# Interleaving two accumulation groups, matmul by matmul, in the value projection and in the memory's key/value projection of a two-layer decoder kernel

## What is computed

```python
mk_p, mv_p = mem_kv(mem_prompt, w_mem_kv[l])    # 256 memory rows -> 512 key and 512 value columns
...
proj = x @ w_in
cb, cc, ch, rq, rk, rv, rg, mq, gl = jnp.split(proj, split_idx, axis=-1)
v = rv.reshape(b, t, RET_HEADS, RET_DV)          # 1024 value columns of the retention branch
q = rotary(rq.reshape(...), pos);  k = rotary(rk.reshape(...), pos) * (RET_DK ** -0.5)
o, new_state = retention(q, k, v, ret_state)
...
m_out = mem_attention(mq.reshape(...), mk, mv).reshape(b, t, MEM_WIDTH) @ w_mem_out
```

## Time and profile before

| | |
|---|---|
| runs of the kernel before | 2145.36, 2146.7, 2146.8 us (median 2146.7) |
| the profiled execution's own time | 2146.93 us |
| its span, from first to last instruction | 2145.1 us |
| PE busy | 2124.1 us (99%) |
| PE's weight loads busy | 2062.7 us (96%) |
| DVE, ACT, POOL busy | 1046.5 (49%), 524.5 (24%), 1310.6 us (61%) |
| mean granted clock of PE | 0.998 |

### The profile page before, as it was taken

The page is one execution under the profiler, slowest core; times in us unless marked ns, Lnnn a source line. Parts: engine busy times, 40 slices in busy tenths (PEclk is TensorE's granted clock), DMA queues, the critical chain, the costliest instruction groups (busy, mean ns, idle before and its releaser), DMA issues.

```text
span 2145.1 us, 38116 instructions
## 1 busy us (share of the span) xinstructions
PE 2124.1 (99%) x15716; PEld 2062.7 (96%) x15716; DVE 1046.5 (49%) x1669; ACT 524.5 (24%) x935; POOL 1310.6 (61%) x1549
## 2 busy tenths in 40 slices
PE   8999999999999999999999999999999999999997
PEld 8898999999999999999998989999999999999997
DVE  6156300543268873626781571006424787726257
ACT  4121021031014141414241210210410141514133
POOL 6744657645683947466757346676456748475574
PEclk9999999999999999999999999999999999999999
DMA  5415324234332323222323153332352313222331
GB/s 175 130 55 171 124 80 137 70 108 155 101 99 60 99 79 99 80 81 80 97 72 118 58 177 107 110 118 70 111 175 79 99 58 101 79 80 79 99 99 45
DMA packets 200315, 215.26 MB, mean 100 GB/s; under 512 B 5600, under 2 KB 192992, under 8 KB 200160
## 3 DMA queue, kind: packets, MB, share of 16 engines
q1 hardware_dynamic: 170688, 172.84, 25.6%
q10 hardware_dynamic: 29472, 40.20, 5.5%
HBM read 199.06 MB, written 13.97 MB: 99 GB/s over the span
## 4 chain that ended last, share of the span: by engine, by line
PE 96%; DVE 3%; ACT 0%; DMA 0%; issue 0%; POOL 0%; ACTq 0%; DVEq 0%
PE gp L578 53%; PE gp L1107 12%; PE gp L604 9%; PE gp L594 7%; PE qb L684 7%; PE gp L758 3%; PE qb L758 2%; PE gp L936 1%; PE gp L948 1%; PE qb L724 1%; DVE r L2157 1%; DVE x_lo L2063 0%; DVE r L2057 0%; DVE r L2054 0%; DVE m_lo L1665 0%; DVE m_hi L1664 0%
## 5 line engine op out<-in xcount | busy, mean ns | idle before, releaser
L466 POOL TENSOR_TENSOR w_lo<-stage,w_hi 128x256 fp32r<-128x256 f32 x1008 | 812.5, 836 | 92.0 <-ACT w_hi L1201 71.7
L463 POOL TENSOR_SCALAR w_hi<-stage 128x1024 fp32r<-128x1024 f32 x240 | 256.1, 1067 | 511.1 <-PE gp L578 257.1
L578 PE MATMUL gp<-b_hi,w_hi 128*128 128x288 f32 x1408 | 303.8, 297 | 0.0
L578 PE MATMUL gp<-x_hi,w_hi 128*128 128x288 f32 x1408 | 303.8, 298 | 0.0
L578 PE MATMUL gp<-x_lo,w_hi 128*128 128x288 f32 x1408 | 301.2, 295 | 0.0
L578 PE MATMUL gp<-x_hi,w_lo 128*128 128x288 f32 x1408 | 301.1, 295 | 0.0
L578 PE MATMUL gp<-b_lo,w_hi 128*128 128x288 f32 x1408 | 300.6, 295 | 0.0
L578 PE MATMUL gp<-b_hi,w_lo 128*128 128x288 f32 x1408 | 300.6, 295 | 0.0
L578 PEld LDWEIGHTS gp<-b_hi,w_hi 128*128 128x128 f32 x1408 | 226.6, 188 | 3.4 <-issue 3.1
L578 PEld LDWEIGHTS gp<-x_hi,w_hi 128*128 128x128 f32 x1408 | 226.8, 189 | 2.9 <-issue 2.6
L578 PEld LDWEIGHTS gp<-x_lo,w_hi 128*128 128x128 f32 x1408 | 226.7, 189 | 0.0
(11 more groups left out here) (299 smaller groups left out, 4272.9 us busy)
## 6 DMA issues: line engine op xcount, KB each, us to landing
stage<-in_w_in SPq DMA_DIRECT2D x54, 1024.0 KB, 5.9
stage<-in_w_up SPq DMA_DIRECT2D x32, 1024.0 KB, 5.4
stage<-in_w_down SPq DMA_DIRECT2D x32, 1024.0 KB, 5.2
stage<-in_w_in SPq DMA_DIRECT2D x40, 256.0 KB, 4.0
stage<-in_w_ret_out SPq DMA_DIRECT2D x8, 1024.0 KB, 5.3
stage<-in_w_mem_kv SPq DMA_DIRECT2D x8, 1024.0 KB, 5.2
stage<-in_w_out SPq DMA_DIRECT2D x8, 1024.0 KB, 5.2
s_in_c<-in_ret_state ACTq DMA_DIRECT2D x8, 512.0 KB, 5.1
```

What stands on the lines that cost most here:

```text
L463: nc.gpsimd.tensor_scalar(hi, raw, 1.0, 1.0, ALU.mult, ALU.mult).then_inc(hi_done, 1)
L466: ins = nc.gpsimd.tensor_tensor(lo[:, k:k + 2, :], raw[:, k:k + 2, :], hi[:, k:k + 2, :].bitcast(F32), ALU.subtract)
L578: last = mm(gp[:, 2 * (i % 2) + half, 0:HALF], w[:, i % 4, k * P:(k + 1) * P], x(k, half), start=(n == 0), stop=(n == 3 * nk - 1))
```

## The change

Nothing is computed that was not before, and no matmul is added or removed. The order of matmuls on PE changes in both projections, and with it the places where PE waits. In V the five token tiles become the groups (1, 2), (3, 4), (0) for `j` = 0 and (3, 1), (2, 4), (0) for `j` = 1, and within a group the two tiles, and so their banks, alternate from one matmul to the next. Among the key tiles, K0 and K1 alternate, then K2 and K3; for these pairs PE first waits for both weight tiles and for both pairs of banks. Among the value tiles the two halves of the memory rows alternate. ACT, DVE, POOL and SP keep their code.

```diff
-                    for t in (1, 2, 3, 4, 0) if j == 0 else (3, 1, 2, 4, 0):
+                    for tiles in ((1, 2), (3, 4), (0,)) if j == 0 else ((3, 1), (2, 4), (0,)):
                         if s == 0:
-                            if j == 0 and t in (1, 3):
-                                pe.wait_ge(pair_free[t // 2], l * (TILES // 2) + T_RV // 2 + 1)
-                            elif j == 0 and t == 0:
-                                take(l, 0, ("v", 0))
-                            elif j == 1 and t in (1, 2, 3):
-                                take(l, (2, 3, 1)[t - 1], ("v", 1))
-                            elif j == 1 and t == 4:
-                                pe.wait_ge(pair_free[1], l * (TILES // 2) + T_RV // 2 + 3)
+                            for t in tiles:
+                                if j == 0 and t in (1, 3):
+                                    pe.wait_ge(pair_free[t // 2], l * (TILES // 2) + T_RV // 2 + 1)
+                                elif j == 0 and t == 0:
+                                    take(l, 0, ("v", 0))
+                                elif j == 1 and t in (1, 2, 3):
+                                    take(l, (2, 3, 1)[t - 1], ("v", 1))
+                                elif j == 1 and t == 4:
+                                    pe.wait_ge(pair_free[1], l * (TILES // 2) + T_RV // 2 + 3)
...
                         for k in (2 * s, 2 * s + 1):
...
-                            for n, (x, w) in enumerate(terms):
-                                last = mm(value_bank(j, t), x, value_rows(w, s, k % 2), start=(k == n == 0),
-                                          stop=(k == KT - 1 and n == len(terms) - 1))
...
+                            for n in range(3 if tiles[0] else 2):
+                                for t in tiles:
...
+                                    end = k == KT - 1 and n == (2 if t else 1)
+                                    last = mm(value_bank(j, t), x, value_rows(w, s, k % 2), start=(k == n == 0), stop=end)
+                                    if end and j == 1 and t in (1, 2, 3):
+                                        last.then_inc(side_full[(2, 3, 1)[t - 1]], 1)
+                                    elif end and t == 4:
+                                        last.then_inc(values_done, 1)
...
             pe.wait_ge(mem_split, l + 1)
-            for i in range(4):
+            for i in (0, 2):
                 t = T_KV + i
-                pe.wait_ge(split_done, l * TILES + t + 1 + RING)
-                pe.wait_ge(pair_free[i % 2], l * (TILES // 2) + t // 2 + 1)
-                n = 0
+                pe.wait_ge(split_done, l * TILES + t + 2 + RING)
+                for bank in range(2):
+                    pe.wait_ge(pair_free[bank], l * (TILES // 2) + t // 2 + 1)
                 for k in range(KT):
-                    for w, x in ((w_hi, mt_hi), (w_hi, mt_lo), (w_lo, mt_hi)):
-                        last = mm(gp[:, 2 * (i % 2), 0:ML], w[:, i, k * P:(k + 1) * P], x[:, k, :],
-                                  start=(n == 0), stop=(n == 3 * KT - 1))
-                        n += 1
-                last.then_inc(tile_done, 1)
+                    for n, (w, x) in enumerate(((w_hi, mt_hi), (w_hi, mt_lo), (w_lo, mt_hi))):
+                        for j in range(2):
+                            last = mm(gp[:, 2 * j, 0:ML], w[:, i + j, k * P:(k + 1) * P], x[:, k, :],
+                                      start=(k == n == 0), stop=(k == KT - 1 and n == 2))
+                            if k == KT - 1 and n == 2:
+                                last.then_inc(tile_done, 1)
             for i in (0, 2):
                 t = T_KV + 4 + i
                 pe.wait_ge(split_done, l * TILES + t + 2 + RING)
                 pe.wait_ge(pair_free[i // 2], l * (TILES // 2) + (T_KV + 4) // 2 + 1)
-                for m in range(2):
-                    n = 0
-                    for k in range(KT):
-                        for x, w in ((mt_hi, w_hi), (mt_hi, w_lo), (mt_lo, w_hi)):
+                for k in range(KT):
+                    for n, (x, w) in enumerate(((mt_hi, w_hi), (mt_hi, w_lo), (mt_lo, w_hi))):
+                        for m in range(2):
```

More of the change, by code:

```diff
@@ L739, in _ @@
                     pe.wait_ge(split_done, l * TILES + T_RV + 4 * j + s + 1 + RING)
-                    for t in (1, 2, 3, 4, 0) if j == 0 else (3, 1, 2, 4, 0):
+                    for tiles in ((1, 2), (3, 4), (0,)) if j == 0 else ((3, 1), (2, 4), (0,)):
                         if s == 0:
-                            if j == 0 and t in (1, 3):
-                                pe.wait_ge(pair_free[t // 2], l * (TILES // 2) + T_RV // 2 + 1)
-                            elif j == 0 and t == 0:
-                                take(l, 0, ("v", 0))
-                            elif j == 1 and t in (1, 2, 3):
-                                take(l, (2, 3, 1)[t - 1], ("v", 1))
-                            elif j == 1 and t == 4:
-                                pe.wait_ge(pair_free[1], l * (TILES // 2) + T_RV // 2 + 3)
-                        first = NS + (t - 1) * P
-                        for k in (2 * s, 2 * s + 1):
[L752 to L756, removed]
-                            for n, (x, w) in enumerate(terms):
-                                last = mm(value_bank(j, t), x, value_rows(w, s, k % 2), start=(k == n == 0),
-                                          stop=(k == KT - 1 and n == len(terms) - 1))
[L760 to L764, removed]
@@ new lines, in _ @@
+                        for k in (2 * s, 2 * s + 1):
+                            for n in range(3 if tiles[0] else 2):
+                                for t in tiles:
+                                    cols = slice(NS + (t - 1) * P, NS + t * P)
+                                    if t == 0:
+                                        x, w = x_short[:, k, :], (w_hi, w_lo)[n]
+                                    else:
+                                        x, w = ((x_hi, x_hi, x_lo)[n][:, k, cols], (w_hi, w_lo, w_hi)[n])
+                                    end = k == KT - 1 and n == (2 if t else 1)
[4 more added lines that the diff above has]
+                                        last.then_inc(values_done, 1)
@@ L943, in _ @@
                 pe.wait_ge(pair_free[i // 2], l * (TILES // 2) + (T_KV + 4) // 2 + 1)
-                for m in range(2):
-                    n = 0
-                    for k in range(KT):
-                        for x, w in ((mt_hi, w_hi), (mt_hi, w_lo), (mt_lo, w_hi)):
+                for k in range(KT):
+                    for n, (x, w) in enumerate(((mt_hi, w_hi), (mt_hi, w_lo), (mt_lo, w_hi))):
+                        for m in range(2):
                             last = mm(gp[:, i + m, 0:2 * P], x[:, k, m * P:(m + 1) * P],
-                                      w[:, i:i + 2, k * P:(k + 1) * P], start=(n == 0), stop=(n == 3 * KT - 1))
-                            n += 1
+                                      w[:, i:i + 2, k * P:(k + 1) * P], start=(k == n == 0), stop=(k == KT - 1 and n == 2))
                 last.then_inc(tile_done, 2)
```

## The result

The changed kernel takes 2160.46 us (2158.9 to 2160.96, 4 runs) against 2146.75 us before: a ratio of 1.0063, 95% interval 1.0051 to 1.0076, 13.7 us slower. The forecast was 2157.5 with a range from 2152.5 to 2161.5. The profiled execution is the quickest of the four, 2158.9 us with a span of 2157.1 us, 12.0 us above that of before.

The account below looks back on a forecast made before the run. PE, busy 99% of the span, was taken as the bound. With 0 for distance and V, KV's 2 x 5.4 = 10.8 us on the profiled 2146.93 gave 2157.7, so 2157.5 us for the median; range 2152.5 to 2161.5.

Parts of the forecast that it names:

- The distance does not change: V and KV: matmuls stay 226.7 and 120.0 ns apart, since alternating banks buys nothing; counted as 0.
- KV: 5.4 us a layer in four gaps: KV: four new PE waits in each layer, 1.1 + 2.4 + 0.7 + 1.2 us.
- The second: Start of K2 and K3: PE waits for ACT's copy of K1, behind ACT's weight tile for M0; 2.4 us.
- The fourth: Start of M2 and M3: PE waits for POOL's low parts of both; 1.1 to 1.2 us.
- third: Start of M0 and M1: PE waits for ACT's copy of K2; 0.7 us, POOL's low part just in time.
- The first gap: Start of K0 and K1: PE waits for DVE's L1869 to leave pair 1; 1.1 us.
- V costs 0: V: the regrouped tiles add no PE wait; cost 0.
- its cover is over 2 us: End of V: outputs(0) has over 2 us to spare behind ACT's later copies; if gone, at most 1 us a layer.
- The clock: Rival: the clock falls in KV's new gaps, about 2.5 us a stretch; 2162.5 with one per layer; chance 5%.
- the worse rate in the 576 matmuls of the MLP: Shifted PE phase may switch 576 matmuls from 130.0 to 133.3 ns: 1.9 us a layer, 3.8 us in the range, unsummed.
- a wait in V that I cost at 0: Rival: only V or KV differs, by a V wait or the worse rate in the 576: 2159 to 2162; chance 7%.
- The rate of stretches: A stretch's matmul distance can differ by 3.3 ns without reason in the code; about 3 us either way, range only.

Follow-up runs that it names:

- experiment 6: Against the kernel before, only the two halves of KV's value tiles alternate; key tiles and V as before: 2146.77 us, ratio 1.000.
- experiment 4: The change's KV with the V of before, and ACT makes both key copies ahead of the two high-part weight tiles: 2155.08 us, ratio 1.0044.
- experiment 5: The change's KV with the V of before, and the four key tiles have four banks of their own: 2152.31 us, ratio 1.0028.
- KV alone: The change's KV with the V of the kernel before: 2158.7 us, ratio 1.0059.
- experiment 7: Kernel before, but in usual tiles (L578, no wait inside) all matmuls of one token half precede the other's, 24 in a row per bank: 2143.66 us.
- experiment 8: Kernel before, but the usual tile (L578) takes its two halves in the order 0, 1, 1, 0: 2157.49 us, ratio 1.0051.
- experiment 9: Kernel before, but in the usual tile (L578) the bank changes after every third matmul: 2150.36 us, ratio 1.0018.
- experiment 10: Kernel before, with 24 matmuls in a row per bank in usual tiles, except 12 first-MLP-group tiles that keep alternating: 2141.23 us, ratio 0.9974.

## Why the prediction was right, and where it was not

- *The distance does not change.* Right, and shown: 226.7 ns in V after the change, 120.0 ns in experiment 6. The 13.3 ns over the columns are there with either order. What they are is not settled.
- *KV: 5.4 us a layer in four gaps.* Right in place, releaser and order, and 5.2 us measured. The sum's terms hold the slower first distance too; with it the gaps are 1.2, 2.2, 0.7 and 1.05 for its 1.1, 2.4, 0.7 and 1.2. The second is shorter since ACT's copy of K1 starts 0.1 us before the end of its weight tile (318.61 against 318.71) and takes 0.36 us, and its release is sooner than I had allowed. The fourth is shorter since POOL's two low parts took 5.60 us (for 5.7). Experiments 4 and 5 show the second, third and fourth causes apart: ACT's written order, then the copies, then the weights of M0 to M3. The first gap, DVE's, is read from the trace and stays in every run with this KV; no experiment removed it.
- *V costs 0.* Wrong. The step that failed is "its cover is over 2 us": I followed what waits for ACT's copies down to `outputs(0)` along `v`, and did not follow DVE, which behind its own addition from `v_low` clears `S`, scales `qd` and makes `sc`, the other operand of the same matmuls. That chain's cover was under 0.1 us. The term is 1.4 us a layer in place of 0; the bound for it, "at most that 1 us", was short too, since `qd` took 1.22 us for 0.69 behind POOL.
- *The clock.* A rival at 5%, and it happens: 1.5 us a time behind the gap of 2.2 us, by the mean clocks in two of four runs of the change and in all of KV alone, but not as often in the change nor as dear as priced. I had set that gap beside an idle of 7.0 us and one of 0.4 us, and no row stood between.
- *Together.* The profiled execution is 12.0 us longer: 2 x 5.2 us in KV and 2 x 1.4 in V, less the 1.4 us won ahead of the first V, and 0.2 us spread over the rest. The median is 13.7 us longer, with a fall of the clock in half of the runs. The forecast had 10.8.
- *The range.* That 2160.46 lies inside it is in part luck. Its upper end stood for the worse rate in the 576 matmuls of the MLP, and these kept their 130.0 ns (74.88 us); what raised the time was the wait in V and the clock, and the sum had neither. The wait in V stood among the rivals, "a wait in V that I cost at 0", at 7%, and the measured median lies in that rival's 2159 to 2162.
- *The rate of stretches.* I had kept it out of the sum as chance. Experiment 5 suggests that it can differ between executions of one program (768 matmuls, 130.0 or 133.3), and in 7 to 10 other orders within a tile brought other rates.

## What to carry to other kernels

Interleaving two groups on PE moves no work, but it moves hand-overs: both banks finish together, both are asked for together, and both weight tiles are freed together, so a double buffer becomes a single one. Where PE is the bound and never waits, compare for each group when it is finished and when it is next asked for, and follow every operand of the first matmul behind it, down each engine's own queue, with what that engine may meet on the way. Measure what the alternation is meant to save first by an edit that moves no wait, such as experiment 6.

## What the runs showed of the hardware that I had not expected

- A matmul of 288 columns takes 130.0, 131.9, 132.5, 133.3 or 134.3 ns in long stretches, at a granted clock of 1.00 and with PE never idle, and the order of its neighbours has a part in it. Halves 0, 1, 0, 1 have two rates, 133.3 and 130.0, in the same stretch of different kernels, and by its times in one and the same program (experiment 5); 24 in a row on one bank give 132.5, halves 0, 1, 1, 0 give 134.3 in most long stretches, the MLP's among them. Over some 8000 matmuls this is worth from -3 to +11 us (experiments 7 and 8), more than most waits here. What picks the rate was not found.
- The clock fell for 3.4 us although PE had been idle for only 2.2 us and was busy again for 1.2 us when it fell; it had also been idle for 1.1 us some 6 us ahead of that gap. With gaps of up to 1.7 us (experiments 4 and 5) the mean clock stayed at 0.998 in 13 runs. In the changed kernel's profile the same gaps left it at 1.00.
- Two instructions that overlapped on DVE (`qd`, two operands from SBUF) and POOL (`w_lo`) did not run side by side: the one that had started 0.1 us later took 0.5 us longer, 1.22 us for 0.69 on DVE, 1.20 for 0.74 on POOL.
